# VectorE makes ten low parts of weight tiles around four norms, three output stages use 256-column triples, and two latent statistics share one PSUM bank

## The chip, the cores and the metric

The kernel runs on one core of one Trainium2 chip. The metric is device time in microseconds, from several runs of the whole program; the profile is one further execution, recorded by the hardware profiler.

## The reference

Two transformer blocks over one sequence of 256 tokens with 1024 channels, all in 32-bit floating point. What matters here:

```python
def rms_norm(x, g, eps=1e-6):
    y = x * rsqrt(mean(x * x, axis=-1) + eps)
    return y * g

# first_block, for l in 0, 1 (l = 0: convolution and memory attention, l = 1: NSA and memory attention)
x = x + mix @ w_out[l]
x = x + square(relu(rms_norm(x, norm_mlp_g[l]) @ w_mlp_in[l])) @ w_mlp_out[l]     # 1024 -> 4096 -> 1024
# at l = 1, from x: kv = rms_norm(x, kv_norm_g) @ w_kv, and h = rms_norm(x, norm_mix_g[1])

# second_block
proj = rms_norm_2(x, g_pre_mix) @ w_in
sb_q, sb_k, sb_v, q_lat, kv_lat, k_rope = split(proj)           # q_lat: 256 channels, kv_lat: 128
o_sb = stick_breaking_attention(sb_q, sb_k, sb_v)
q = rms_norm_2(q_lat, g_q_lat) @ w_q_up
kv = rms_norm_2(kv_lat, g_kv_lat) @ w_kv_up
# MLA attention, output projection, a convolved GELU MLP, and a gated embedding follow
```

## The kernel before

**Layout.** Channels lie on partitions, tokens along the free dimension: x is 8 tiles of 128 channels by 256 tokens. A weight matrix is read in blocks of 1 MB into a ring of four (SyncE's queue); a block holds two weight tiles, each of which gives 128 output channels from up to 8 k-steps. WEIGHT_TILES numbers them through the kernel; they are 280.

**Exact products from parts.** Each fp32 operand is split into a high part, rounded to fp32r, and a low part, the rest. ScalarE makes a weight tile's high part (`split_high`, L618); the low part is a subtraction of 128x1024 elements (`split_low`, L626) on VectorE or GpSimd, as LOW_ENGINE, made by `low_part_engines`, says. Four slots (SPLIT) of parts are in flight: the parts of tile w + 4 are made once TensorE is through with tile w; `pump(stage, t)` stands in the queues of ScalarE and VectorE for that. GpSimd makes its own with `low_parts` in the order of the tiles.

**Two forms of a k-step on TensorE.** `linear` issues a triple of 256-column matmuls: high x high, high x low, low x high (`product`). `linear_halves` issues two: the high weights against both parts of the activation side by side (512 columns), and the low weights against the high part (256 columns); the output then stands in two halves of the bank that have to be added (`half_products`).

**Banks.** Six PSUM banks are used in turn, in the order of `psum_tiles()`: tile n takes bank n mod 6 once tile n - 6 has been emptied. All matmuls are recorded at L758 (`mm`), transposes at L928.

**The four norms.** Behind out0, mlp_out0, out1 and mlp_out1 an RMS norm of x follows (mlp0, mix1, mlp1, smix), whose factor is put in behind the next product. `residual` on VectorE goes through the 8 output tiles:

```python
                for t in range(KD):
                    add_output(stage, first + t)
                    if t >= 1:
                        low_of_x(t - 1, hi, lo, gname, name)
                        fold(name, t - 1)
                        pump(stage, first + t - 1)
                low_of_x(KD - 1, hi, lo, gname, name)
                fold(name, KD - 1)
                pump(stage, first + KD - 1)
```

add_output adds the two halves to x's tile; ScalarE (`squares_of_x`) then makes the tile's high part and its square and runs its own pump; low_of_x makes the low part, for which the next stage's first tile waits k-step by k-step (`linear(..., arriving)`); fold sums the squares. Between chunks the MLP's back products (mlp_out tiles 0 to 23) use add_output as well. After two tiles of the next stage TensorE sums the squares into the statistic, ScalarE takes the root, VectorE the reciprocal, TensorE broadcasts it.

**The latent stage.** Behind the stick sums (`stick_sums`) TensorE makes s_lat 0 (the kv latent), the statistic of the q latent, s_lat 1 (the rotary key), the statistic of the kv latent, the first token half of s_val 0, and both broadcasts, then a swap of the rotary key, the second token half, and the query heads. ScalarE has the logs of four heads (a table load for Ln), pumps and squares, then two roots (another table load); VectorE has `stick_keeps`, the scaled latents and two reciprocals (`invert`). The query heads wait until VectorE has read the q latent's broadcast.

Of the kernel before, what the change touches and what calls it, by code (L numbers as in the profile page):

```python
# [218 lines left out]
def psum_tiles():  # L219
# [110 lines left out]
        linear("s_in", 1, t)  # L330
    linear("sb.Z", 1, 7)
    linear("sb.C", 4)
    linear("s_lat", 1)
    linear("qlat.stat", 1)
    linear("s_lat", 1, 1)
    linear("kvlat.stat", 1)
    linear("qlat.bc", 1)
    linear("kvlat.bc", 1)
    linear("krope.swap", 1)
# [69 lines left out]


GATE_SUMMED = 14
ON_GPSIMD = (("ple_gate", 2), ("ple_gate", 3))


def low_part_engines():

    out = []
    for w, (_, _, (stage, t)) in enumerate(WEIGHT_TILES):
        beside_conv = w >= SPLIT and (stage in ("a_in", "mem_kv0", "mem_kv1") or (stage == "out0" and t < 2))
        beside_sticks = w % 2 == 1 and (stage in ("s_lat", "s_val") or (stage == "s_in" and t >= SPLIT))  # L420
        out.append("gpsimd" if beside_conv or beside_sticks or (w >= SPLIT and w % 4 == 1 and stage not in ("b_in", "up") and (stage, t) != ("out0", 3)
                                                             and (stage, t) != ("ple_gate", 1))
                   or (stage, t) in ON_GPSIMD else "vector")
    return out

# [11 lines left out]
def build(nc, x_in, mem_in, p_in, pos_in, consts_in, weights_in, out):  # L437
    ctx = ExitStack()
    with ctx:
# [304 lines left out]
        def _(pe):  # L744
# [390 lines left out]
            def mlp(name, into, back, signal, sizes, per, act):  # L1135
                for n in range(len(sizes) + 1):
                    if n == 0 and per == 2:
                        dst = take(f"{name}.stat", 0)
                        for k in range(KD):
                            arriving_squares(name, dst, k)  # L1140
                        full_bcast(name)
                        linear(into, 0, sizes[0] * per, act, f"{name}.act")
                    elif n == 0:
                        linear_halves(into, 0, 2, act, f"{name}.act")
                        folded_stat(name)
                        linear_halves(into, 2, 1, act)
                        full_bcast(name)
                        linear_halves(into, 3, sizes[0] * per - 3, act)
                    elif n < len(sizes) and per == 1:
                        linear_halves(into, KD * n * per, sizes[n] * per, act)  # L1150
                    elif n < len(sizes):
                        linear(into, KD * n * per, sizes[n] * per, act)
                    if n >= 1:

                        pe.wait_ge(sem(signal), KD * (n - 1) + sizes[n - 1])
                        linear_halves(back, KD * (n - 1), KD, hidden_parts[:, :, (n - 1) % 2, :, :])

            def block_ready(name, r=0):
                b = BLOCK_AT[name, r, 0]
# [212 lines left out]
                    wait_out_emptied(pe, ("nsa", tt, g))  # L1372
            for tt in range(TT):
                wait_out_emptied(pe, ("mem1", "mem", tt, 0))
            linear_halves("out1", 0, KD, act_parts)
            mlp_block(1)


# [63 lines left out]
            pe.wait_ge(sem("sb.below"), 1)  # L1442
            for h in range(4):
                stick_sums(h)
            linear("s_lat", 0, 1, projected)
            full_stat("qlat", 2, signal=1)
            linear("s_lat", 1, 1, projected)
            full_stat("kvlat", 1, src=sq[:, 2:3, :], signal=1)
            linear_tokens("s_val", 0, 2, projected, (0,))
            full_bcast("qlat")  # L1450
            full_bcast("kvlat")
# [108 lines left out]
        def _(act):  # L1560
# [437 lines left out]
            for t in range(2):  # L1998
                wait_emptied(act, "s_in", 8 + t)
            do(flat(sq[:, 0:2, :]), flat(lat[:, 0:2, :]), ACT.Square).then_inc(sem("qlat.squares"), 1)  # L2000
            stick_logs(range(4, 8))
            pump("s_lat", 0)
            wait_emptied(act, "s_lat", 0)
            do(sq[:, 2, :], lat[:, 2, :], ACT.Square).then_inc(sem("kvlat.squares"), 1)
            pump("s_lat", 1)
            root("qlat", 2, 256)
            root("kvlat", 2, 128)
            token_pair("s_val", 0, sbv[:, :, 0:256], "smix")
            keep_queries(range(4))
            stick_weights(range(4, 8))  # L2010
# [207 lines left out]
        def _(dve):  # L2218
# [48 lines left out]
                stt(lo[:, t, :], x[:, t, :], const(gname, t, 1), hi[:, t, :].bitcast(F32), ALU.mult, ALU.subtract)\  # L2267
                    .then_inc(sem(f"{name}.act"), 1)

            def add_output(stage, t):  # L2270
                wait_tile(dve, stage, t)
                settle(tt_(x[:, t % KD, :], x[:, t % KD, :], bank(stage, t)[:, 0:SEQ], ALU.add))
                tt_(x[:, t % KD, :], x[:, t % KD, :], bank(stage, t)[:, SEQ:2 * SEQ], ALU.add).then_inc(emptied(stage, t), 1)

# [20 lines left out]
            def residual(stage, first, hi, lo, gname, name):  # L2295

                for t in range(KD):
                    add_output(stage, first + t)
                    if t >= 1:
                        low_of_x(t - 1, hi, lo, gname, name)  # L2300
                        fold(name, t - 1)
# [4 lines that stand above are left out]
# [631 lines left out]
            pump("s_lat", 0)  # L2937
            stick_keeps((4, 5))
            scaled(("s_lat", 1), krope[64:96, :], bank("s_lat", 1)[64:96, 0:SEQ], rb[64:96, :])
            pump("s_lat", 1)  # L2940
            invert("qlat", 2)
            invert("kvlat", 2)
            stick_keeps((6, 7))
            wait_tile(dve, "qlat.bc", 0)
            for t in range(2):
# [370 lines left out]
```

## Time and profile before

| | |
|---|---|
| runs, median | 1050.36 us |
| runs, lowest and highest of 3 | 1049.38, 1052.92 us |
| profiled execution | 1048.86 us, of which span 1047.0 us |
| TensorE matmul busy | 989.5 us (95%) |
| VectorE busy | 783.5 us (75%) |
| ScalarE busy | 610.1 us (58%) |
| GpSimd busy | 205.7 us (20%) |
| mean granted clock of TensorE | 0.982 |
| low parts (L626) | 206 on VectorE, 74 on GpSimd |

Shares are of the span. A matmul row's duration reaches over the start of the next one, because matmuls are pipelined: the distance from start to start is the pace, and the duration is longer. The same holds, less, for VectorE and ScalarE. In a timeline an idle time in brackets is that of the engine before the row, with what ended it. The granted clock is 1.00 at 2.4 GHz and 0.50 at 1.2 GHz.

### The profile page before, as it was taken

To read this page: it belongs to the slowest core of one execution; us is meant where nothing else is said; L and a number is where in the kernel's file an instruction comes from. 1 tells how busy PE (TensorE), PEld (TensorE's weight loads), DVE (VectorE), ACT (ScalarE), POOL (GpSimd) and SP (SyncE) were. 2 spreads that over 40 slices of the span, in tenths; PEclk is the share of its full clock that TensorE was granted. 3 is DMA by queue.
4 is the path that set the end of the run, shared out by engine and by line. 5 is a ranking of instruction groups with operands and counts; after the bars stand their busy time and mean duration, and the time that the engine had idled before them with its cause. 6 is when DMAs were issued, how large, how long until landed. Compare 5 with 4: busy or idle time off the path is not lost.

```text
span 1047.0 us, 17720 instructions
## 1 busy us (share of the span) xinstructions
PE 989.5 (95%) x6807; PEld 885.7 (85%) x6807; DVE 783.5 (75%) x1446; ACT 610.1 (58%) x1143; POOL 205.7 (20%) x109
## 2 busy tenths in 40 slices
PE   4999999999999996899999999999999999999986
PEld 4978888888889885788878888897798999999875
DVE  4888789876868768877987677666576788768775
ACT  5634557564645867645547455574565665545555
POOL 2953112122111001001212211222000000202151
PEclk9999999999999999999999999998998999999998
DMA  9481154555544440034455454521405354554601
GB/s 379 168 239 57 66 201 162 203 200 176 190 176 183 167 161 1 1 142 167 175 201 201 166 202 162 197 85 46 161 6 197 122 190 176 203 187 154 219 1 41
DMA packets 24995, 160.49 MB, mean 153 GB/s; under 512 B 2768, under 2 KB 5072, under 8 KB 6608
## 3 DMA queue, kind: packets, MB, share of 16 engines
q1 hardware_dynamic: 24048, 155.69, 41.1%
q10 hardware_dynamic: 864, 3.66, 0.9%
q8 instruction: 55, 0.90, 0.4%
q14 instruction: 28, 0.23, 0.1%
HBM read 157.86 MB, written 1.49 MB: 152 GB/s over the span
## 4 chain that ended last, share of the span: by engine, by line
PE 77%; DVE 14%; ACT 4%; issue 4%; DMA 1%; DVEq 0%; ACTq 0%
PE bank L758 73%; DVE split_lo L626 2%; PE obank L758 2%; PE bank L928 1%; ACT split_hi L618 1%; DVE tmp L2240 1%; DVE mlp_parts L2240 1%; DMA consts<-in_consts 1%; DVE x L2232 1%; DVE rowmax L2790 1%; ACT L1570 1%; DVE hidden_parts L2232 1%; DVE tmp L2232 1%; DVE act_parts L2232 1%; DVE probs L2236 0%
## 5 line engine op out<-in xcount | busy, mean ns | idle before, releaser
L618 ACT ACTIVATE split_hi<-ring 128x1024 fp32r<-128x1024 f32 (+1 forms) x280 | 290.0, 1049 | 117.4 <-PE bank L758 116.9
L758 PE MATMUL bank<-act_parts,split_hi 128*128 128x256 f32 (+1 forms) x1632 | 317.8, 293 | 23.0 <-DVE split_lo L626 13.4
L626 POOL TENSOR_TENSOR split_lo<-ring,split_hi 128x1024 fp32r<-128x1024 f32 (+1 forms) x74 | 180.6, 2450 | 704.0 <-ACT split_hi L618 703.9
L758 PEld LDWEIGHTS bank<-act_parts,split_hi 128*128 128x128 f32 x1632 | 256.4, 191 | 33.1 <-issue 24.2
L626 DVE TENSOR_TENSOR split_lo<-ring,split_hi 128x1024 fp32r<-128x1024 f32 (+1 forms) x206 | 250.7, 1227 | 41.0 <-ACT split_hi L618 40.3
L758 PE MATMUL bank<-hidden_parts,split_hi 128*128 128x512 f32 (+1 forms) x816 | 267.1, 379 | 5.5 <-DVE split_lo L626 2.5
L758 PE MATMUL bank<-act_parts,split_lo 128*128 128x256 f32 x880 | 247.8, 282 | 0.0
L758 PE MATMUL bank<-hidden_parts,split_lo 128*128 128x256 f32 x752 | 210.8, 280 | 0.0
L758 PEld LDWEIGHTS bank<-hidden_parts,split_hi 128*128 128x128 f32 x816 | 149.8, 189 | 37.5 <-DVE split_lo L626 3.1
L758 PE MATMUL bank<-mlp_parts,split_hi 128*128 128x512 f32 x512 | 178.8, 392 | 2.1 <-DVE mlp_parts L2240 2.1
L758 PEld LDWEIGHTS bank<-act_parts,split_lo 128*128 128x128 f32 x880 | 167.4, 190 | 0.0
L758 PE MATMUL bank<-mlp_parts,split_lo 128*128 128x256 f32 x512 | 144.3, 282 | 0.0
L758 PEld LDWEIGHTS bank<-hidden_parts,split_lo 128*128 128x128 f32 x752 | 141.8, 189 | 0.0
L758 PEld LDWEIGHTS bank<-mlp_parts,split_hi 128*128 128x128 f32 x512 | 96.1, 188 | 23.0 <-DVE mlp_parts L2240 2.9
L758 PEld LDWEIGHTS bank<-mlp_parts,split_lo 128*128 128x128 f32 x512 | 96.8, 189 | 0.0
L2232 DVE TENSOR_TENSOR x<-x,bank 128x256 f32<-128x256 f32 x160 | 67.0, 419 | 37.7 <-PE bank L758 34.4
L2240 DVE SCALAR_TENSOR_TENSOR tmp<-bank,consts,tmp 128x255 f32<-128x255 f32 (+1 forms) x88 | 39.7, 476 | 29.3 <-ACT tmp L1570 29.2
L2232 DVE TENSOR_TENSOR tmp<-bank,tmp 128x256 f32<-128x256 f32 x64 | 27.0, 422 | 37.9 <-ACT tmp L1573 35.4
L1570 ACT ACTIVATE tmp<-bank,consts 128x256 f32<-128x256 f32 x45 | 25.3, 563 | 47.2 <-PE bank L758 47.1
L1570 ACT ACTIVATE tmp<-tmp 128x256 f32<-128x256 f32 x64 | 26.8, 418 | 28.5 <-DVE tmp L2240 26.2
L2232 DVE TENSOR_TENSOR hidden_parts<-tmp,hidden_parts 128x256 fp32r<-128x256 f32 x64 | 41.3, 660 | 0.0
L1570 ACT ACT_TABLE_LOAD x29 | 37.2, 1283 | 4.3 <-issue 3.8
(285 smaller groups left out, 1245.5 us busy)
## 6 DMA issues: line engine op xcount, KB each, us to landing
ring<-in_weights SPq DMA_DIRECT2D x141, 1024.0 KB, 4.8
ring<-in_weights SPq DMA_DIRECT2D x5, 768.0 KB, 4.3
shifted<-conv_rows SPq DMA_DIRECT2D x9, 142.0 KB, 4.4
x<-in_x ACTq DMA_DIRECT2D x1, 1024.0 KB, 7.8
y<-in_mem ACTq DMA_DIRECT2D x1, 1024.0 KB, 9.8
out<-x SPq DMA_DIRECT2D x4, 256.0 KB, 2.6
consts<-in_consts ACTq DMA_DIRECT2D x1, 933.0 KB, 13.1
ring<-in_weights SPq DMA_DIRECT2D x1, 512.0 KB, 3.5
```

Of the source, the lines that this page charges most:

```text
L618: nc.scalar.activation(split_hi[:, w % SPLIT, 0:n], src, ACT.Copy).then_inc(sem("high_parts"), 1)
L626: (nc.vector if engine == "vector" else nc.gpsimd).tensor_tensor(split_lo[:, w % SPLIT, 0:n], src, split_hi[:, w % SPLIT, 0:n].bitcast(F32 ...
L758: return nc.tensor.matmul(dst, lhsT, rhs, start=start, stop=stop)
L928: return nc.tensor.transpose(dst, src, const("ident")[0:k, 0:k])
L1570: return nc.scalar.activation(dst, src, func, bias=bias, scale=scale, **more)
L2232: return nc.vector.tensor_tensor(dst, a, b, op)
L2240: return nc.vector.scalar_tensor_tensor(out=dst, in0=a, scalar=s, in1=b, op0=op0, op1=op1)
L2790: settle(nc.vector.reduce_max(rowmax[:, c:c + m], bank("nsa", "S", n)[:, :].rearrange("p (s k) -> p s k", k=u.keys), X_AXIS, negate=True))
```

## The change

Three edits. (1) Ten weight tiles near the four norms get their low part from VectorE instead of GpSimd. (2) out1 and the last eight tiles of mlp_out0 and mlp_out1 are made as 256-column triples (`linear`), and the add on VectorE is a single one there; out0 and the other tiles of mlp_out keep the halves. (3) Both latent statistics are written to one bank behind s_lat 1, as four columns; ScalarE squares the kv latent before the logs; both roots follow one wait, and both reciprocals stand before pump("s_lat", 1). psum_tiles() has one tile fewer, so that the banks of all later tiles shift by one.

```diff
-    linear("s_lat", 1)
-    linear("qlat.stat", 1)
-    linear("s_lat", 1, 1)
-    linear("kvlat.stat", 1)
+    linear("s_lat", 2)
+    linear("lat.stat", 1)
...
+LAST_BACK = KD * (len(MLP_CHUNKS) - 1)
+BESIDE_NORMS = {(stage, t) for l in range(2) for stage, first, n in ((f"out{l}", 4, 4), (f"mlp_in{l}", 0, 4), (f"mlp_out{l}", LAST_BACK, 8))
+                for t in range(first, first + n)} | {(stage, t) for stage in ("kv", "s_in") for t in range(4)}
...
+        beside_norms = (stage, t) in BESIDE_NORMS
...
-                                                             and (stage, t) != ("ple_gate", 1))
+                                                             and (stage, t) != ("ple_gate", 1) and not beside_norms)
...
-                        linear_halves(back, KD * (n - 1), KD, hidden_parts[:, :, (n - 1) % 2, :, :])
+                        if per == 1 and n == len(sizes):
+                            linear(back, KD * (n - 1), KD, chunk_of((n - 1) % 2))
+                        else:
+                            linear_halves(back, KD * (n - 1), KD, hidden_parts[:, :, (n - 1) % 2, :, :])
...
-            linear_halves("out1", 0, KD, act_parts)
+            linear("out1", 0, KD, projected)
...
-            linear("s_lat", 0, 1, projected)
-            full_stat("qlat", 2, signal=1)
-            linear("s_lat", 1, 1, projected)
-            full_stat("kvlat", 1, src=sq[:, 2:3, :], signal=1)
+            linear("s_lat", 0, 2, projected)
+            pe.wait_ge(sem("qlat.squares"), 1)
+            pe.wait_ge(sem("kvlat.squares"), 1)
+            dst = take("lat.stat", 0)
+            for tt in range(TT):
+                for k in range(3):
+                    c = 2 * (k // 2) + tt
+                    last = mm(dst[:, c:c + 1], sq[:, k, 128 * tt:128 * tt + 128], const("ones", 0, 1), k != 1, k >= 1)
+            ready(last)
...
             do(flat(sq[:, 0:2, :]), flat(lat[:, 0:2, :]), ACT.Square).then_inc(sem("qlat.squares"), 1)
+            wait_emptied(act, "s_lat", 0)
+            do(sq[:, 2, :], lat[:, 2, :], ACT.Square).then_inc(sem("kvlat.squares"), 1)
             stick_logs(range(4, 8))
             pump("s_lat", 0)
-            wait_emptied(act, "s_lat", 0)
-            do(sq[:, 2, :], lat[:, 2, :], ACT.Square).then_inc(sem("kvlat.squares"), 1)
             pump("s_lat", 1)
-            root("qlat", 2, 256)
-            root("kvlat", 2, 128)
+            wait_tile(act, "lat.stat", 0)
+            for n, (name, dim) in enumerate((("qlat", 256), ("kvlat", 128))):
+                c = RC[name]
+                ins = do(smalls[:, c:c + 2], bank("lat.stat", 0)[:, 2 * n:2 * n + 2], ACT.Sqrt, const("eps6"), 1.0 / dim)
+                if n:
+                    ins.then_inc(emptied("lat.stat", 0), 1)
...
-            def add_output(stage, t):
+            def add_output(stage, t, whole=False):
                 wait_tile(dve, stage, t)
+                if whole:
+                    tt_(x[:, t % KD, :], x[:, t % KD, :], bank(stage, t)[:, 0:SEQ], ALU.add).then_inc(emptied(stage, t), 1)
+                    return
                 settle(tt_(x[:, t % KD, :], x[:, t % KD, :], bank(stage, t)[:, 0:SEQ], ALU.add))
                 tt_(x[:, t % KD, :], x[:, t % KD, :], bank(stage, t)[:, SEQ:2 * SEQ], ALU.add).then_inc(emptied(stage, t), 1)
...
-                    add_output(stage, first + t)
+                    add_output(stage, first + t, stage != "out0")
...
             scaled(("s_lat", 1), krope[64:96, :], bank("s_lat", 1)[64:96, 0:SEQ], rb[64:96, :])
+            wait_emptied(dve, "lat.stat", 0)
+            for name in ("qlat", "kvlat"):
+                assert inverted[inversions[0]] == name
+                inversions[0] += 1
+                nc.vector.reciprocal(rc[:, RC[name]:RC[name] + 2], smalls[:, RC[name]:RC[name] + 2]).then_inc(sem("inverted"), 1)
             pump("s_lat", 1)
-            invert("qlat", 2)
-            invert("kvlat", 2)
             stick_keeps((6, 7))
```

## Rows read from the trace of the kernel before

**Rows 1.** The page's part 4, shares of the chain by engine.
```profile
PE 77%; DVE 14%; ACT 4%; issue 4%; DMA 1%; DVEq 0%; ACTq 0%
```

**Rows 2.** TensorE's timeline, the first matmul after each norm's wait: start, duration.
```profile
145.37 0.50 PE L758 MATMUL bank<-mlp_parts,split_hi 128*128 128x512 f32 x1 [0.83 <-DVE mlp_parts L2240]
...
325.82 0.39 PE L758 MATMUL bank<-hidden_parts,split_hi 128*128 128x256 f32 x1 [0.72 <-DVE hidden_parts L2240]
...
477.58 0.50 PE L758 MATMUL bank<-mlp_parts,split_hi 128*128 128x512 f32 x1 [1.25 <-DVE mlp_parts L2240]
...
661.88 0.51 PE L758 MATMUL bank<-act_parts,split_hi 128*128 128x256 f32 x2 [1.24 <-DVE act_parts L2240]
```

**Rows 3.** The latent stage: timelines of TensorE, ScalarE, VectorE, and a window (the clock is PEclk).
```profile
710.42 0.55 PE L758 MATMUL bank<-split_hi,act_parts 128*128 128x256 f32 x1 [2.00 <-ACT smalls L1570]
...
715.68 1.33 PE L758 MATMUL bank<-consts,rc 128*128 128x128 f32 x8
...
720.48 3.62 PE L758 MATMUL bank<-temps,ring 128*96 128x256 f32 x16
...
703.44 1.28 ACT L1570 ACT_TABLE_LOAD   x1
...
707.36 0.40 ACT L1570 ACTIVATE sq<-temps 128x256 f32<-128x256 f32 x1
...
710.02 0.41 ACT L1570 ACTIVATE smalls<-bank,consts 128x2 f32<-128x2 f32 x2
...
703.48 0.42 DVE L2232 TENSOR_TENSOR temps<-bank,rb 128x256 f32<-128x256 f32 x1 [1.13 <-PE bank L758]
...
709.10 2.71 DVE L2240 SCALAR_TENSOR_TENSOR decays<-sq,decays 128x384 f32<-128x384 f32 x1
...
714.01 0.23 DVE L2249 RECIPROCAL rc<-smalls 128x2 f32<-128x2 f32 x2
...
709.43:716.26 6.83, 5.84 (x27) 5.87 (x28) 6.63 (x13) 0.99 (x3) 1.96 (x1) 0.50 0.42 154
```

**Rows 4.** VectorE's timeline, last tile of mlp_out0.
```profile
322.63 0.88 DVE L2232 TENSOR_TENSOR x<-x,bank 128x256 f32<-128x256 f32 x2
323.42 0.48 DVE L2240 SCALAR_TENSOR_TENSOR hidden_parts<-x,consts,hidden_parts 128x256 fp32r<-128x256 f32 x1
323.82 0.42 DVE L2232 TENSOR_TENSOR square_sum<-square_sum,sq 128x256 f32<-128x256 f32 x1
324.15 1.22 DVE L626 TENSOR_TENSOR split_lo<-ring,split_hi 128x1024 fp32r<-128x1024 f32 x1
325.29 0.48 DVE L2240 SCALAR_TENSOR_TENSOR hidden_parts<-x,consts,hidden_parts 128x256 fp32r<-128x256 f32 x1
```

**Rows 5.** TensorE's timeline, last matmul of a k-step: first and last of 65, 51 and 47 steps.
```profile
452.33 0.28 PE L758 MATMUL bank<-act_parts,split_lo 128*128 128x256 f32 x1
...
474.86 0.28 PE L758 MATMUL bank<-mlp_parts,split_lo 128*128 128x256 f32 x1
...
304.11 0.28 PE L758 MATMUL bank<-hidden_parts,split_lo 128*128 128x256 f32 x1
...
321.96 0.28 PE L758 MATMUL bank<-hidden_parts,split_lo 128*128 128x256 f32 x1
...
776.12 0.28 PE L758 MATMUL bank<-act_parts,split_lo 128*128 128x256 f32 x1
...
792.73 0.28 PE L758 MATMUL bank<-act_parts,split_lo 128*128 128x256 f32 x1
```

**Rows 6.** VectorE's and GpSimd's timelines, tile 6 of the last mlp_out1 chunk.
```profile
656.21 2.22 DVE L2240 SCALAR_TENSOR_TENSOR act_parts<-x,consts,act_parts 128x256 fp32r<-128x256 f32 x1
...
655.75 2.40 POOL L626 TENSOR_TENSOR split_lo<-ring,split_hi 128x1024 fp32r<-128x1024 f32 x1 [9.18 <-ACT split_hi L618]
```

**Rows 7.** TensorE's wait behind the feed-forward norm, and the window behind it.
```profile
1006.92 0.77 PE L758 MATMUL bank<-act_parts,split_hi 128*128 128x256 f32 x2 [4.51 <-DVE act_parts L2240]
...
1006.40:1009.80 3.40, 2.88 (x13) 2.91 (x14) 3.40 (x7) 2.56 (x9) 2.59 (x4) 0.50 0.00 0
```

## The prediction

> **What bounds the kernel.** I read first the chain that ended last, by engine: TensorE holds 77% of it and VectorE 14% [rows 1]. So work moved between VectorE and GpSimd counts only where TensorE waits for it, and I looked next at TensorE's timeline at the five places that the diff touches. Around each of the four norms TensorE stops once, at the same place: the last of the eight k-steps of the first tile behind the norm waits for the low part of x's tile 7. The waits are 0.83, 0.72, 1.25 and 1.24 us [rows 2], 4.04 us together: more than that the norms cannot give, 0.4% of the kernel. In the latent stage it waits once for 2.00 us, for the square root of the first statistic [rows 3].
>
> **Why the norms' waits have two sizes.** VectorE's timeline at the end of the first block's MLP is the undisturbed case [rows 4]. The two halves of x += output start at 322.63, low_of_x(6) at 323.42, the fold of squares at 323.82, the low part of a weight tile (pump) at 324.15, low_of_x(7) at 325.29, and TensorE goes on at 325.82. The adds thus take 0.79 us of VectorE's queue, a low_of_x 0.40, a fold 0.33, a weight tile's low part 1.14: 2.66 us a tile. TensorE, without a wait, would have gone on 0.72 earlier, at 325.10. A tile of TensorE is 8 steps of 0.347 us in out1 [rows 5], 2.77 us, so VectorE has only 0.11 us a tile with which to catch up. At the end of the second MLP it is disturbed [rows 6]: GpSimd's low part starts at 655.75, the low_of_x issued at 656.21 lasts 2.22 us instead of 0.48 and ends with it. Both of its tensor operands lie in SBUF, as do GpSimd's. That iteration has no pump, so the net loss is 1.74 - 1.14 = 0.60 us, two tiles before the end, and 0.11 a tile cannot repay it. Thus 1.24 instead of 0.72.
>
> **Low parts moved to VectorE.** By the rule in low_part_engines ten tiles change sides: out0 7, mlp_in0 3, mlp_out0 27 and 31, kv 3, out1 5, mlp_in1 1, mlp_out1 25 and 29, s_in 1. Each costs VectorE 1.14 us [rows 4], 11.4 us in all, and takes a GpSimd piece of 2.4 us away [rows 6]. Hardly any of it is on the path alone: mlp_out0 27 and mlp_out1 25 fall into an iteration in which VectorE has time to spare, mlp_in0 3, kv 3 fall behind low_of_x(7), where the next thing that TensorE wants from VectorE is two tiles away; the rest each replace a stall, 1.74 us in the one shown, by 1.14.
>
> **One add instead of two.** With triples the product is whole in columns 0 to 255 and add_output is one operation: 0.33 us of the queue, as the fold shows [rows 4], instead of 0.79, so 0.46 saved on the last tile of three stages, and the iteration falls to 2.20 us against TensorE's 2.77: VectorE then meets every tile as it ends, and nothing that happened earlier is left at the end. For the three triple stages the wait is then 0.72 - 0.46 = 0.26 us. What remains is the pump of tile 6, which stands in VectorE's queue ahead of low_of_x(7); the triples don't move it. Savings: 0.46 at mlp_out0, 0.99 at out1, 0.98 at mlp_out1. out0 keeps its halves, and only loses its stall: 0.83 to 0.72, 0.11. Together 2.54 us. If VectorE does not catch up in any of them, the stages save only the 0.46 each, 1.4 us; the other bound is the whole 4.04.
>
> **Triples on TensorE.** Both forms stream 768 columns a step, but three matmuls and three weight loads instead of two of each. 24 tiles of 8 steps are 192 steps. Halves in out1: 452.33 to 474.86 for 65 steps, 0.3467 us; halves in mlp_out0: 304.11 to 321.96 for 51, 0.3500; triples in o: 776.12 to 792.73 for 47, 0.3533 [rows 5]. Low bound: nothing, since the columns are the same. High bound, all at o's pace: 64 x 0.0066 + 128 x 0.0033 = 0.85 us. I take 0.5, about the middle, since the halves' own pace varies between stages by as much as the difference.
> The Trainium skill ("TensorE: Matmul & The Clock Gate", section "Wait — 56ns, not 53.3ns?") speaks against this edit: each matmul costs about 2.5 ns beyond its columns. By that, as an estimate, 192 more matmuls would cost 0.48 us. The difference of 3.3 to 6.6 ns a step between the rows is of that order.
>
> **The latents.** Before [rows 3]: s_lat 0, its statistic, s_lat 1, its statistic, and then s_val waits for a bank that the root of qlat.stat empties at 710.02, behind a table load. With the new numbering s_val 0 takes the bank of s_lat 0, which VectorE empties at once. So TensorE runs on: s_lat 1 from 703.3, where s_lat 0 ends (VectorE picks it up at 703.48), with no statistic in front, until 706.1; six one-column products for some 0.8 us (eight broadcast products take 1.33), s_val's first half of 2.85 us (24 matmuls at 0.118 us, a third of o's step [rows 5]) to about 709.8. Then it needs the reciprocals. ScalarE now squares the kv latent before the logs, and for that waits until VectorE has scaled s_lat 0 (703.48 + 0.42 = 703.90): with the square's 0.40 the logs' table load starts at 704.3, 0.85 us later than 703.44; the square taken out behind them gives about 0.3 back. All that follows on ScalarE is 0.55 us later: the high part that frees GpSimd's s_val 3, and the roots. On VectorE the stall behind that GpSimd piece (2.71 us at 709.10) ends 0.55 later too, and the reciprocals move from 714.01 to about 714.56. Behind the waiting reciprocals only stick_keeps((6, 7)) is queued, which is wanted after 720. The broadcast starts at 714.66 instead of 715.68, and to the query heads it is as before 4.80 us (715.68 to 720.48), less 0.29 for the half clock that ended in it: 719.2, a gain of 1.3 us.
> But TensorE is then idle for 4.9 us, and comes back cold. In the stage before the clock was granted at 0.50 from 709.43 to 716.26, behind a pause of 2 us [rows 3]; behind a later wait of 4.51 us until 1006.92, it was 0.50 (1.2 GHz) until 1009.8, 2.88 us busy [rows 7]. Half of 2.88, 1.44 us, is what that stretch costs; where it starts earlier, about 1 us. I take 1.3: gain and loss cancel, latents 0. Bounds: -1.3 with the clock full, +1.0 if two stretches follow (4.6 us of work at half).
>
> **Sum.** Against the profiled execution, 1048.86 us (span 1047.0): -2.54 + 0.5 + 0.0 = -2.0, so 1046.8. It ran 1.5 us below the median of the runs shown, 1050.36; against that, 1048.3 us.
>
> **Rivals.** 1. *The moved wait costs more than the removed one.* TensorE's one pause of 4.9 us brings two slow stretches; latents +1.0, total -1.0: 1049.3. For it: one pause of 2 us already had a slow stretch twice as long as the one at 1006.4. Against it: the longer pause there had only one. The same page of the Trainium skill, section "Why this matters for your kernels", warns of long pauses between bursts of matmuls, because the clock falls; by it the removal of a 2 us wait is not worth a pause of 4.9. The trace agrees that it falls.
> 2. *The clock stays up*, or the slow stretch falls into the pause. Latents -1.3, total -3.3: 1047.0. Against it: both pauses shown, of 2.00 and of 4.51 us, have a slow stretch behind them.
> 3. *Slower than before.* The slow stretch starts just as TensorE comes back and is as long as before, 6.83 us, all of it over dense products: it costs 3.4 instead of 1.3, latents +2.1; with the triples at their high bound (+0.85) the total is -2.54 + 0.85 + 2.1 = +0.4: 1050.8. It decides from a slow stretch of about 6 us of work on; two unlucky ones also elsewhere would be needed to pass +0.3%.
> 4. *VectorE is not what holds the norms.* If low_of_x(7) waits for ScalarE's high part, or the waits come back in the next tile, the four give only the triples' cost: total +0.5: 1050.9. Against it: all four waits are ended by VectorE's low_of_x [rows 2], which follows on its pump without a gap [rows 4].
>
> **How the numbers follow.** Forecast 0.45, rival 1 0.2, rival 2 0.15, rival 3 0.08, rival 4 0.12. 0.3% is 3.15 us, about what a measurement of this kernel tells from no change; the three runs before spread over 3.5 us. Faster by more means below 1047.2: rival 2 mostly, and the lower end of the forecast (norms at their 4.04 bound), 0.25. Slower by more, above 1053.5, needs rival 3 or 4 and an execution with more slow stretches: 0.1. The same: 0.65. The range goes from the forecast with 4.04 for the norms and -1.0 for the latents (1050.36 - 4.5 = 1045.8) to rivals 3 and 4, 1051.0. The forecast's own range is 1047.0 to 1049.6.
>
> **What would show it.** Right: the norms' waits in TensorE's timeline at 0.2 to 0.4 us in three, 0.7 in the first; no VectorE operation of over 1.3 us in the four stages but the low parts; GpSimd with 64 instead of 74 low parts; the step of the triples at 0.350 to 0.354; in the latent stage no wait between the statistic and s_val, one wait of 4 to 5.5 us before the broadcast, and a slow clock behind it. Wrong: if the wait behind out1 stays above 1 us (then VectorE doesn't catch up), if the steps exceed 0.357 (then the third weight load is not hidden), or if the reciprocals come after 716.

## The result, and the profile after

| | before | after |
|---|---|---|
| median of 12 runs each | 1050.36 us | 1054.47 us |
| lowest and highest | 1048.20, 1052.92 | 1052.36, 1056.58 |
| ratio, 95% interval | | 1.0043 [1.0034, 1.0052] |
| profiled execution (span) | 1048.86 (1047.0) | 1054.04 (1052.2) |
| mean granted clock of TensorE | 0.982 | 0.978 |
| low parts on VectorE, on GpSimd | 206, 74 | 216, 64 |

The changed kernel is slower by 4.1 us, and lies outside the predicted range. The profiled executions differ by 5.2 us.

First the part of the page that the prediction began with, the shares of the chain, after (TensorE had 77% in [rows 1]):

```profile
PE 81%; DVE 11%; ACT 3%; issue 3%; DMA 1%; DVEq 0%; ACTq 0%
```

TensorE's share of the chain has risen by 4 points, and by the two pages its matmuls are busy for 996.8 us where they were for 989.5. It is idle for 2 us less and still takes longer: the time is lost while TensorE works.

**The norms.** TensorE's timeline, the first matmul after each norm's wait, after:

```profile
146.22 0.50 PE L760 MATMUL bank<-mlp_parts,split_hi 128*128 128x512 f32 x1 [0.81 <-DVE mlp_parts L2254]
...
326.85 0.50 PE L760 MATMUL bank<-hidden_parts,split_hi 128*128 128x256 f32 x2 [0.26 <-DVE hidden_parts L2254]
...
478.06 0.50 PE L760 MATMUL bank<-mlp_parts,split_hi 128*128 128x512 f32 x1 [0.34 <-DVE mlp_parts L2254]
...
662.02 0.50 PE L760 MATMUL bank<-act_parts,split_hi 128*128 128x256 f32 x2 [0.32 <-DVE act_parts L2254]
```

They were 0.83, 0.72, 1.25 and 1.24 [rows 2], 4.04 us; now 1.73. The waits give back 2.31 us. VectorE's timeline at the end of the second MLP shows why, against [rows 4, 6]:

```profile
659.28 0.42 DVE L2246 TENSOR_TENSOR x<-x,bank 128x256 f32<-128x256 f32 x1 [0.59 <-PE bank L760]
659.62 0.48 DVE L2254 SCALAR_TENSOR_TENSOR act_parts<-x,consts,act_parts 128x256 fp32r<-128x256 f32 x1
660.02 0.42 DVE L2246 TENSOR_TENSOR square_sum<-square_sum,sq 128x256 f32<-128x256 f32 x1
660.35 1.22 DVE L628 TENSOR_TENSOR split_lo<-ring,split_hi 128x1024 fp32r<-128x1024 f32 x1
661.49 0.48 DVE L2254 SCALAR_TENSOR_TENSOR act_parts<-x,consts,act_parts 128x256 fp32r<-128x256 f32 x1
```

The single add starts 0.59 us after VectorE ran dry: it waits for the tile to end. There is one add where two stood, and the low part of a weight tile (660.35, the pump of tile 6) is what is left ahead of low_of_x(7).

**The triples' steps.** TensorE's timeline, last matmul of a k-step, after: first and last of 55 steps in mlp_out0, 65 in out1 and 49 in mlp_out1.

```profile
303.99 0.28 PE L760 MATMUL bank<-hidden_parts,split_lo 128*128 128x256 f32 x1
...
323.80 0.28 PE L760 MATMUL bank<-hidden_parts,split_lo 128*128 128x256 f32 x1
...
452.95 0.28 PE L760 MATMUL bank<-act_parts,split_lo 128*128 128x256 f32 x1
...
475.70 0.28 PE L760 MATMUL bank<-mlp_parts,split_lo 128*128 128x256 f32 x1
...
641.33 0.28 PE L760 MATMUL bank<-hidden_parts,split_lo 128*128 128x256 f32 x1
...
658.97 0.28 PE L760 MATMUL bank<-hidden_parts,split_lo 128*128 128x256 f32 x1
```

The steps are 0.3602, 0.3500 and 0.3600 us; as halves they were 0.3500 in mlp_out0 and 0.3467 in out1 [rows 5], and 0.3500 in mlp_out1 too (before, 640 to 657 us). That is 128 x 0.010 + 64 x 0.0033 = 1.5 us, where the prediction had 0.5 and a high bound of 0.85. Waits and steps together: a gain of 0.8 us.

**The latents.** TensorE's, ScalarE's and VectorE's timelines after, and windows over two stretches at the lower clock (busy time of the engines, then the granted clock, DMA share and GB/s):

```profile
715.37 2.05 PE L760 MATMUL bank<-consts,rc 128*128 128x128 f32 x8 [4.84 <-DVE rc L2961]
...
722.76 2.54 PE L760 MATMUL bank<-temps,ring 128*96 128x256 f32 x11
...
704.06 0.42 ACT L1580 ACTIVATE sq<-temps 128x256 f32<-128x256 f32 x1 [0.53 <-DVE temps L2246]
704.49 1.28 ACT L1580 ACT_TABLE_LOAD   x1
...
710.76 0.41 ACT L1580 ACTIVATE smalls<-bank,consts 128x2 f32<-128x2 f32 x2
...
703.60 0.42 DVE L2246 TENSOR_TENSOR temps<-bank,rb 128x256 f32<-128x256 f32 x1 [1.15 <-PE bank L760]
...
708.53 1.23 DVE L628 TENSOR_TENSOR split_lo<-ring,split_hi 128x1024 fp32r<-128x1024 f32 x1 [4.51 <-ACT split_hi L620]
709.67 2.71 DVE L2254 SCALAR_TENSOR_TENSOR decays<-y,decays 128x384 f32<-128x384 f32 x1
...
715.06 0.23 DVE L2961 RECIPROCAL rc<-smalls 128x2 f32<-128x2 f32 x2
...
714.70:721.50 6.80, 6.13 (x24) 5.23 (x25) 5.65 (x15) 0.00 (x0) 0.78 (x1) 0.50 0.21 88
...
769.40:776.20 6.80, 6.80 (x35) 6.80 (x34) 3.38 (x11) 2.60 (x6) 0.00 (x0) 0.50 0.01 2
```

The pause before the broadcast is there, 4.84 us, as worked out. But the broadcast starts at 715.37, not 714.66, and the query heads at 722.76, not 719.2; before they started at 720.48 [rows 3]. From the broadcast to the heads it takes 7.39 us, where it took 4.80. The slow stretch begins as the pause ends (714.70) and TensorE is busy for 6.13 of its 6.80 us; in [rows 3] it began at 709.43. A second one of 6.80 us lies in the output projection, all of it dense products. No window at half clock lay there in the profiled execution of before.

Laid matmul by matmul against the profiled execution of before, TensorE is late by

| at (us, before) | 100 | 690 | 730 | 760 | 830 | 1002 |
|---|---|---|---|---|---|---|
| late by (us) | 0.9 | 0.1 | 2.3 | 2.3 | 4.4 | 5.1 |

The 0.9 us stand there before the first tile that the diff touches, and the profiled executions of the other kernels below lie between -0.5 and +0.9 us there, so they are not the change's. From 100 to 690 the norms and steps give the 0.8 us back that their rows give. The latent stage loses 2.2 us and the output projection 2.1, and 0.7 come in the feed-forward block, whose code is unchanged but for the numbers of the banks. Its steps are 0.3533 us in a part of it where they were 0.3500, as they are in the profiled execution of e9 below too, which has before's banks.

### The profile page after: what moved, and what is told of

Same layout as the page of the kernel before. It is cut to its first block, busy times and chain, and to the rows that moved or that the text cites. A ratio compares the mean times of both kernels' runs of the same rounds, so it can differ in the third digit from the quotient of the medians.

```text
span 1052.2 us, 18079 instructions
## 1 busy us (share of the span) xinstructions
PE 996.8 (95%) x6999; PEld 901.5 (86%) x6999; DVE 770.6 (73%) x1432; ACT 610.3 (58%) x1143; POOL 181.4 (17%) x99
## 4 chain that ended last, share of the span: by engine, by line
PE 81%; DVE 11%; ACT 3%; issue 3%; DMA 1%; DVEq 0%; ACTq 0%
PE bank L760 78%; PE obank L760 3%; DVE split_lo L628 2%; PE bank L930 1%; DVE tmp L2254 1%; DMA consts<-in_consts 1%; DVE rowmax L2807 1%; DVE hidden_parts L2246 1%; DVE tmp L2246 1%; ACT split_hi L620 1%; DVE probs L2250 0%; DVE pt_lo L2246 0%; ACT L1580 0%; DVE y L2246 0%; ACT probs L1580 0%
## 5 line engine op out<-in xcount | busy, mean ns | idle before, releaser
L760 PE MATMUL bank<-act_parts,split_hi 128*128 128x256 f32 (+1 forms) x1696 | 321.3, 290 | 21.9 <-DVE split_lo L628 13.3
L628 DVE TENSOR_TENSOR split_lo<-ring,split_hi 128x1024 fp32r<-128x1024 f32 (+1 forms) x216 | 262.7, 1225 | 44.5 <-ACT split_hi L620 43.9
L760 PEld LDWEIGHTS bank<-act_parts,split_hi 128*128 128x128 f32 x1696 | 266.2, 192 | 29.1 <-issue 24.1
L628 POOL TENSOR_TENSOR split_lo<-ring,split_hi 128x1024 fp32r<-128x1024 f32 (+1 forms) x64 | 155.8, 2445 | 697.1 <-ACT split_hi L620 696.9
L760 PEld LDWEIGHTS bank<-hidden_parts,split_hi 128*128 128x128 f32 x944 | 165.1, 189 | 31.4 <-DVE split_lo L628 3.1
L2246 DVE TENSOR_TENSOR x<-x,bank 128x256 f32<-128x256 f32 x136 | 57.0, 419 | 45.5 <-PE bank L760 43.2
```

The lines of the kernel that those rows point to most:

```text
L628: (nc.vector if engine == "vector" else nc.gpsimd).tensor_tensor(split_lo[:, w % SPLIT, 0:n], src, split_hi[:, w % SPLIT, 0:n].bitcast(F32 ...
L760: return nc.tensor.matmul(dst, lhsT, rhs, start=start, stop=stop)
L2246: return nc.vector.tensor_tensor(dst, a, b, op)
```

## The experiments

In each, "mean" is the mean time of the runs compared; before, in the same batches, had medians of 1050.16, 1050.04 and 1050.81 us and means of 1050.23, 1050.22 and 1050.78 us (29 to 35 runs each). Each of the three batches is compared with its own, and the change with the 12 runs of before beside it (mean 1050.30); the differences below are of means. Such a difference is uncertain by about 1 us either way, e1's by 2.

**One part at a time: e1 (edit 3), e2 (edits 1 and 2), e3 (edit 1), e9 (edit 2).** The edits are hunks of the diff above, put on the kernel before. e9, as it differs from the kernel before (the hunk of mlp_out and the body of add_output are as above):

```diff
...
-            linear_halves("out1", 0, KD, act_parts)
+            linear("out1", 0, KD, projected)
...
-                    add_output(stage, first + t)
+                    add_output(stage, first + t, stage != "out0")
```

> The kernel before with the third edit alone (both latent statistics in one bank). Theory A: the latent edit is where the time went. TensorE's pause of 5 us before the broadcast brings a slow stretch of 6.8 us over dense products, and a further slow stretch follows in the output projection (from 769 us in the changed kernel); together 2.1 + 2.3 us and a little more behind it: 4 to 5.5 us over before, ratio 1.004 to 1.005. Rival B: the further slow stretch is chance of one execution or comes of the norm edits; then only the 2.1 us of the latent stage, ratio about 1.002. Rival C: the latents cost nothing and the norm edits are to blame: 1.000.

> The kernel before with the first two edits alone (low parts on VectorE, triples), old latent stage. Theory A: the waits shrink from 4.04 to about 1.7 us and the triples give 1.5 us back (0.360 instead of 0.350 us a step in both mlp_out stages, 0.350 instead of 0.347 in out1), so 0.6 to 0.9 us under before, ratio 0.999 to 1.000. Rival C: the norm edits are to blame, ratio above 1.002.

> The kernel before with the first edit alone: ten low parts on VectorE, halves everywhere. The waits behind out1 and mlp_out1 fall from 1.25 to about 0.72 us, since no GpSimd piece stalls VectorE there, and no triple costs anything: 1.1 us under before, ratio 0.999, and at least as good as with the triples. If VectorE does not catch up with two adds a tile, the waits stay near 1.2 and the ratio at 1.000.

> Edit 2 alone (triples in out1 and the last eight tiles of both mlp_outs; the ten low parts stay on GpSimd, the latent stage is the old one). Theory (the stalls behind GpSimd's pieces and the two half adds were separate costs that add up; the triples' steps cost 1.3 us at 0.360 and 0.2 us at 0.350): the norms' waits 0.83, 0.26, about 0.3 to 0.8 and 0.8, since with 0.57 us to spare a tile VectorE catches up one stall of 1.7 us only in three tiles; total -1.9 + 1.5 = -0.4 us, 1049.8. Rival (triples are the whole gain of the two edits, low parts give nothing): same waits as with both edits, 0.83, 0.26, 0.34, 0.32, total -0.8 or better, since the ten low parts don't cost VectorE anything: 1049.3. Second rival (the triples' slower steps eat more than the waits give): above 1050.5.

| | median us | ratio [95%] | mean, less before's |
|---|---|---|---|
| e1, latents | 1055.53 | 1.0042 [1.0025, 1.0059] | +4.3 |
| e2, low parts and triples | 1048.98 | 0.9993 [0.9984, 1.0002] | -0.8 |
| e3, low parts | 1051.11 | 1.0005 [0.9996, 1.0015] | +0.5 |
| e9, triples | 1050.67 | 1.0001 [0.9988, 1.0014] | 0.0 |
| the change (its own 12 runs of before) | 1054.47 | 1.0043 [1.0034, 1.0052] | +4.2 |

The latent edit alone makes the kernel as slow as the whole change does. Edits 1 and 2 come out as the 0.8 us that the profile's rows give, though the interval still holds 1, so that they gain anything isn't shown. e1's figures rest on six runs, and its profiled one is the fastest of them (1051.39, clock 0.981); its slowest took 1056.84 at 0.976. The clocks differ by 0.005. As the clock has two levels, 1.00 and 0.50, that is 10.5 us more of the 1050 at half clock; half of it, 5.25, is nearly the 5.45 us between the two. TensorE's wait and a window in e1's trace:

```profile
715.17 2.05 PE L756 MATMUL bank<-consts,rc 128*128 128x128 f32 x8 [4.84 <-DVE rc L2951]
```

```profile
713.50:723.70 10.20, 8.53 (x36) 7.58 (x37) 6.62 (x17) 0.11 (x1) 1.88 (x1) 0.52 0.22 93
```

The same pause, and a slow stretch of 10.2 us. It begins at 713.0, half a microsecond ahead of the window shown, so TensorE is busy for some 8 us of it. e1's trace, laid against before's, loses 2.9 us in the latent stage and nothing more up to 805, with the banks numbered as in the change: that shift costs nothing there.

TensorE's norm waits in e3:

```profile
145.95 0.51 PE L762 MATMUL bank<-mlp_parts,split_hi 128*128 128x512 f32 x1 [0.81 <-DVE mlp_parts L2244]
...
326.41 0.50 PE L762 MATMUL bank<-hidden_parts,split_hi 128*128 128x256 f32 x2 [0.72 <-DVE hidden_parts L2244]
...
477.84 0.50 PE L762 MATMUL bank<-mlp_parts,split_hi 128*128 128x512 f32 x1 [0.81 <-DVE mlp_parts L2244]
...
661.63 0.51 PE L762 MATMUL bank<-act_parts,split_hi 128*128 128x256 f32 x2 [0.78 <-DVE act_parts L2244]
```

and in e9, with VectorE's and GpSimd's operations at tile 6 of the last mlp_out1 chunk:

```profile
145.82 0.50 PE L758 MATMUL bank<-mlp_parts,split_hi 128*128 128x512 f32 x1 [0.83 <-DVE mlp_parts L2243]
...
326.45 0.50 PE L758 MATMUL bank<-hidden_parts,split_hi 128*128 128x256 f32 x2 [0.26 <-DVE hidden_parts L2243]
...
477.14 0.50 PE L758 MATMUL bank<-mlp_parts,split_hi 128*128 128x512 f32 x1 [0.36 <-DVE mlp_parts L2243]
...
661.45 0.50 PE L758 MATMUL bank<-act_parts,split_hi 128*128 128x256 f32 x2 [0.32 <-DVE act_parts L2243]
...
656.17 2.07 DVE L2243 SCALAR_TENSOR_TENSOR act_parts<-x,consts,act_parts 128x256 fp32r<-128x256 f32 x1
...
655.55 2.40 POOL L626 TENSOR_TENSOR split_lo<-ring,split_hi 128x1024 fp32r<-128x1024 f32 x1 [9.42 <-ACT split_hi L618]
```

Either edit removes what the stalls left: the low parts alone take the waits to 0.72 to 0.81, the triples alone to 0.26 to 0.36, with the stall of 2.07 us still there. With the single add VectorE has time to repay it before the last tile. Beside the triples the ten low parts give 0.04 us of waits (1.77 against 1.73). The low parts for themselves save 4.04 - 3.12 = 0.92 us of waits, but the runs of e3 don't show it: +0.5, and its interval, down to 0.9996, excludes a gain of 0.92 us. What took it back is open. e9's waits and steps give 0.8 us by the rows, and its runs 0.0, which is within their uncertainty.

**e8: the triples in out1 only,** with edit 1 (mlp_out keeps its halves: the step of 0.360 and its 1.3 us go). As it differs from e2:

```diff
-                        if per == 1 and n == len(sizes):
-                            linear(back, KD * (n - 1), KD, chunk_of((n - 1) % 2))
-                        else:
-                            linear_halves(back, KD * (n - 1), KD, hidden_parts[:, :, (n - 1) % 2, :, :])
+                        linear_halves(back, KD * (n - 1), KD, hidden_parts[:, :, (n - 1) % 2, :, :])
...
-                    add_output(stage, first + t, stage != "out0")
+                    add_output(stage, first + t, stage == "out1")
```

> The kernel before with the first edit and triples in out1 alone; mlp_out keeps its halves. If the dear step (0.360 instead of 0.350 us) belongs to the triples of mlp_out, the two last mlp_out chunks give 1.3 us back and cost 0.46 us each in longer waits: 0.3 to 0.4 us under the two norm edits together (0.9993), ratio 0.998 to 1.000. If the step stays at 0.360 there, it has another cause.

1050.39 us, 1.0004 [0.9992, 1.0016], mean +0.2. The halves of mlp_out are back at 0.350 us a step, but the waits behind them at 0.72 and 0.78. What the step costs and what the wait gives (1.3 us against 0.92) lie too close for the runs to tell them apart: e8 was expected below e2 and isn't, and it settles nothing more.

**e4: the pause filled with the kernel's own work.** On the changed kernel, both token halves of s_val 0 stand ahead of the broadcasts.

```diff
+    linear("s_val", 1)
...
-    linear("s_val", 1)
...
-            linear_tokens("s_val", 0, 2, projected, (0,))
+            linear_tokens("s_val", 0, 2, projected)
...
-            linear_tokens("s_val", 0, 2, projected, (1,))
```

> The changed kernel with the second token half of s_val 0 moved ahead of the broadcasts (and its bank taken there), so that 2.9 us of products stand in TensorE's pause of 5 us. Theory A: the pause falls to about 2 us, another of 1.5 to 2 us stands before the query heads, which start 2 us earlier than in the kernel before, and the long slow stretch shrinks or goes: 3 to 6 us under the changed kernel, ratio 0.997 to 1.000. Rival B (the stretch in the output projection is not tied to the pause): 2 to 3 us under it, ratio 1.001 to 1.002. Rival C: no change from the changed kernel, 1.004.

1050.64 us, 1.0004 [0.9996, 1.0013]; mean +0.1, so 4.1 us less than the change. TensorE's timeline and a window of e4:

```profile
713.46 1.13 PE L760 MATMUL bank<-consts,rc 128*128 128x128 f32 x8 [2.04 <-DVE rc L2960]
716.98 5.05 PE L760 MATMUL bank<-temps,ring 128*96 128x256 f32 x16 [1.79 <-DVE temps L2253]
```

```profile
716.40:719.80 3.40, 2.82 (x7) 1.96 (x8) 3.20 (x7) 0.38 (x1) 0.99 (x1) 0.51 0.00 0
```

TensorE does the same work and still stands for 3.83 us, instead of 4.84, but in two pieces of 2, and the lower clock lasts 3.40 us instead of 6.80. One microsecond less of waiting comes with 4 us less of time; the rest is put down to the clock, for which the means over all runs below speak too.

**e5 and e6: the pause filled with work that nobody needs.** 20 products of 512 columns (bf16, constant operands) go into the bank of the broadcast before it is made; e5 has edit 3 alone, e6 is the whole change. The work of the kernel is unchanged.

```diff
-                if name in ("ffn", "postffn", "postple"):
-                    keep_busy(dst, {"postple": 3 * (1 - again)}.get(name, 4))
+                if name in ("ffn", "postffn", "postple", "qlat"):
+                    keep_busy(dst, {"postple": 3 * (1 - again), "qlat": 20}.get(name, 4))
```

> The kernel before with the latent edit alone, and 20 needless 512-column products of constants in TensorE's pause before the q broadcast (about 4.4 us at full clock; they write the bank that the broadcast then overwrites). Theory A: the pause is what lowers the clock, and the slow stretches behind it, not the pause, are what the edit costs. With TensorE occupied the clock stays at 1.00 from 707 to 720, the query heads start 1 to 1.5 us earlier than before, and the runs come to 0 to 2 us under before, 4 to 6 us under the latent edit alone (1.0042): ratio 0.998 to 1.000. Rival D: the latent edit costs time by its later chain (reciprocals and what waits for them): the ratio stays at 1.003 to 1.004 although the clock is full.

> The changed kernel with the same 20 needless products in the pause. Theory A: the norm edits' gain (0.8 us in the mean) comes on top: 1 to 2.5 us under before, ratio 0.9975 to 0.999. Rival D: 1.003 to 1.004, as the changed kernel.

| | median us | ratio [95%] | mean, less before's | the same without the fill |
|---|---|---|---|---|
| e5 | 1052.51 | 1.0021 [1.0007, 1.0035] | +1.9 | +4.3 (e1) |
| e6 | 1050.32 | 0.9999 [0.9988, 1.0010] | -0.1 | +4.2 (the change) |

TensorE's timeline in e5, and windows of e6:

```profile
711.36 4.49 PE L756 MATMUL bank<-cbias_b,ident_b 128*128 128x512 bf16 x20
716.27 1.16 PE L756 MATMUL bank<-consts,rc 128*128 128x128 f32 x8 [0.42 <-DVE rc L2951]
```

```profile
710.30:715.20 4.90, 4.58 (x23) 1.92 (x21) 4.77 (x9) 0.88 (x3) 1.69 (x1) 1.00 0.39 139
715.20:722.00 6.80, 6.70 (x44) 5.75 (x45) 5.26 (x15) 1.87 (x4) 1.26 (x1) 1.00 0.13 55
765.50:772.30 6.80, 6.80 (x34) 6.80 (x34) 3.36 (x11) 2.59 (x5) 0.00 (x0) 0.50 0.00 0
```

Twenty products that serve nothing take 4.3 us off the whole change, clearly, and 2.4 off the latent edit, only just beyond the runs' uncertainty. Both kernels were expected below before's time, and neither is. The products end no wait earlier: the broadcast of e6 starts at 715.30, 0.07 from where it did without them. Only the clock differs, 1.00 where it was 0.50, and from the broadcast to the query heads e6 takes 4.63 us and e5 4.62, where the change took 7.39:

```profile
719.93 3.62 PE L760 MATMUL bank<-temps,ring 128*96 128x256 f32 x16
```

The last window shows what the fill doesn't reach, the slow stretch in the output projection.

**What the new order is worth at full clock.** Against the profiled execution of before, TensorE passes the latent stage (690 to 730) 0.7 us sooner in e6 and in e5. But that execution is the odd one. In those of e2, e3, e8, e9 and e10, whose latent stage is the same as before's, the slow stretch behind the same pause lasted 3.40 us instead of 6.83, and the stage passed 1.1 us sooner than in before's. e2's, as an example:

```profile
709.35 0.43 PE L762 MATMUL bank<-split_hi,act_parts 128*128 128x256 f32 x1 [2.01 <-ACT smalls L1577]
...
709.50:712.90 3.40, 3.40 (x17) 3.40 (x18) 3.30 (x6) 0.00 (x0) 0.82 (x1) 0.50 0.36 104
```

Against these five the new order gains nothing by 730 even with its pause filled, and unfilled it loses 3.3 us in the profile of the change and 4.1 in e1's, not 2.2 and 2.9.

**e7: the stall beside GpSimd's s_val 3 taken away.** On the changed kernel VectorE makes the low part of s_val 3, behind the reciprocals.

```diff
-        beside_sticks = w % 2 == 1 and (stage in ("s_lat", "s_val") or (stage == "s_in" and t >= SPLIT))
+        beside_sticks = w % 2 == 1 and (stage, t) != ("s_val", 3) and (stage in ("s_lat", "s_val") or (stage == "s_in" and t >= SPLIT))
...
-                                                             and (stage, t) != ("ple_gate", 1) and not beside_norms)
+                                                             and (stage, t) not in (("ple_gate", 1), ("s_val", 3)) and not beside_norms)
```

> The changed kernel with the low part of s_val 3 made by VectorE (behind the reciprocals) instead of GpSimd, so that no GpSimd piece holds up stick_keeps((4, 5)) in front of the reciprocals. The reciprocals come 2 us earlier and TensorE's pause falls from 5.0 to about 3 us. Theory A: both the chain and the cold clock get shorter, 2 to 4 us under the changed kernel, ratio 1.000 to 1.002. If the clock falls for a pause of 3 us as for one of 5, only 1 to 2 us: 1.002 to 1.003.

1050.96 us, 1.0013 [1.0000, 1.0026]; mean +1.3, so 2.9 us less than the change. TensorE's timeline and a window:

```profile
714.84 1.13 PE L760 MATMUL bank<-consts,rc 128*128 128x128 f32 x8 [2.68 <-DVE rc L2961]
```

```profile
716.40:719.80 3.40, 3.40 (x16) 3.05 (x16) 3.30 (x8) 0.00 (x0) 0.00 (x0) 0.53 0.77 277
```

Without the stall of 2.71 us the pause shrinks by 2.16 us, and 3.40 us at the lower clock follow in place of 6.80. The time falls by 2.9 us, which is the pause's 2.16 within the runs' uncertainty.

**The clock over all runs.** Each run has a mean granted clock, and with levels of 1.00 and 0.50 it gives the time at the lower one. As an estimate, that time costs half of itself at most, where all of it falls on dense products. The runs compared here are of different batches in part.

| | mean clock | us at the lower clock |
|---|---|---|
| before, in the three batches | 0.9796, 0.9801, 0.9792 | 42.7, 41.8, 43.6 |
| the change; e1; e7 | 0.9769; 0.9775; 0.9768 | 48.6; 47.4; 48.6 |
| e4; e5; e6 | 0.9800; 0.9805; 0.9815 | 41.9; 41.1; 38.7 |

e6 has 9.9 us less of it than the change, at most 5.0 us of time (measured 4.3); e5 6.3 less than e1, at most 3.1 (2.4); e4 6.7 less than the change, 3.4 and the wait's 1.0 together 4.4 (4.1). e7 has no less than the change: over all its runs only the shorter pause is seen. e1 has 4.7 us more than before, at most 2.4 of its 4.3 us; the rest fits a slow stretch that fell partly into the pause before and falls on dense products now. e5 has no more than before, so its +1.9 us are not explained by longer slow stretches.

**e10 and e11: a second fill.** 28 dummy products instead of 10 ahead of the gate (ple_gate, the first product behind the feed-forward norm), where TensorE stood for 4.51 us [rows 7]; e10 on e2, e11 on e6.

```diff
-            keep_busy(take("ple_gate", 0), 10)
+            keep_busy(take("ple_gate", 0), 28)
```

> Edits 1 and 2 with the old latent stage, and 28 instead of 10 dummy products of 512 columns (0.22 us each) ahead of the first gate product, where TensorE otherwise stands for about 4.5 us at about 1002. They are the candidate for the fastest version. Theory (what a pause costs is the slow clock over the dense work behind it): the slow stretch at about 1003 to 1007 goes, half of 2.9 us of busy time at half clock is saved, -1.4 us against the 1048.98 of the two edits alone: 1047.6 by the median. Rival (the clock falls for another reason, or the fill ends later than VectorE's low part and delays the product): no change or up to +0.5, 1049 to 1049.5.

> The changed kernel with both fills: 20 dummy products in the latent stage's pause of 5 us and 28 instead of 10 ahead of the gate. Theory: 1050.3 of the changed kernel with the first fill alone, less 1.4 us for the clock behind the second: 1048.9; it stays 0.5 to 1.5 us above the version with the old latent stage and the same second fill. Rival (the latents' new order is worth what was hoped once no clock is lost): at or below that version.

| | median us | ratio [95%] | mean, less before's |
|---|---|---|---|
| e10 | 1049.99 | 0.9991 [0.9979, 1.0002] | -0.9 |
| e11 | 1048.52 | 0.9985 [0.9973, 0.9998] | -1.9 |

TensorE's timeline in e11, and windows:

```profile
999.42 6.21 PE L760 MATMUL bank<-cbias_b,ident_b 128*128 128x512 bf16 x28
1006.27 0.47 PE L760 MATMUL bank<-act_parts,split_hi 128*128 128x256 f32 x2 [0.64 <-DVE act_parts L2254]
```

```profile
714.20:722.00 7.80, 7.77 (x49) 6.55 (x50) 6.26 (x14) 2.94 (x6) 1.95 (x2) 1.00 0.12 51
1006.27:1013.07 6.80, 6.71 (x53) 6.30 (x54) 6.80 (x10) 3.70 (x10) 5.55 (x6) 1.00 0.00 0
```

Behind both former pauses the clock is full, where [rows 7] show 0.50. e11 is the one version whose interval lies wholly below before's time, by 0.15%. The two give the second fill a different worth: e10 is at e2's difference (-0.9 against -0.8), where 1.4 less were expected, e11 1.8 us below e6's; but that is within the uncertainty of four means. e11's place against e10 (1.0 us lower) is within what these runs leave uncertain.

## Why the prediction was wrong

**The norms' waits: right in the trace.** Predicted 0.72 and three of 0.26, measured 0.81, 0.26, 0.34 and 0.32: 2.31 us instead of 2.54. The reason for the single add was right too (VectorE meets every tile as it ends). That a stall makes the difference between 0.7 and 1.25 was right as well: e3, without stalls but with two adds, waits 0.81 and 0.78 there. What the sum gave to the low parts on top of the single add was not theirs: e9 has nearly the same waits without them.

**The triples' steps: mis-sized.** 0.5 was taken and 0.85 was the high bound, from the step of o. Measured is 1.5 us, nearly all of it at 0.360 us a step in mlp_out, above the mark of 0.357 at which the prediction called itself wrong. That mark stood for a third weight load that isn't hidden; whether that is the cause wasn't tested, and the same form runs at 0.350 in out1. The Trainium skill's 2.5 ns for each matmul ("TensorE: Matmul & The Clock Gate", section "Wait — 56ns, not 53.3ns?"), weighed in the prediction, would have been too little as well: a step of one more matmul is 10 ns longer in mlp_out and 3.3 in out1.

**The latents: the step that failed.** "I take 1.3: gain and loss cancel, latents 0." The wait of 4.9 us was right (4.84). The start of the reciprocals was 0.5 late (715.06, not 714.56): the 0.3 us that taking out the later square gives back never reaches VectorE, whose unbroken chain from the low part at 708.53 to the reciprocals (6.53 us, before 6.52) starts behind the weight tile ahead of that square. The broadcast follows them by 0.31 us, not 0.10. Then the size of the slow stretch, which is the greater part. The prediction took its cost, 1.3, from the 2.88 us of busy time behind the later pause [rows 7], though the row for this very stage had a stretch of 6.83 [rows 3]. Measured are stretches of 6.80 and 10.20 us over dense products. From the broadcast to the heads the change takes 7.39 us and e6, at full clock, 4.63, so the clock costs 2.8, and the stage stands 2.2 us behind where it stood before, beyond the upper bound of 1.0. That is rival 3's mechanism, and its figure for this stage (+2.1). It had a chance of 0.08, because it was tied to the triples' high bound and to a stretch longer than the one of [rows 7]; yet the triples passed that bound, and the length stood in [rows 3]. The Trainium skill's warning of long pauses between bursts of matmuls (same page, section "Why this matters for your kernels"), named there beside rival 1, agrees with what the runs show here: 4.3 us between the pause and the same pause filled.

**The sum.** With what was measured it is -2.3 + 1.5 + 2.2 = +1.4, not -2.0: that alone would have made the kernel slower, but only by about a quarter of what the profiles differ by (5.2). The rest of that, 0.9 at the start, 2.1 in the output projection and 0.7 in the feed-forward block, stands where the diff changes nothing, or nothing but the numbers of the banks, and no term had it. The sum also leaned on one execution of before whose latent stage was 1.1 us slower than in the five other profiles with the same stage.

**Shown and not shown.** Shown: the latent edit is the loss (e1 against e2), and the slow clock behind the pause is most of it (e6: idle time replaced by dummy products, the wait's end unmoved, -4.3 us; e5 and e4 support it, e7 doesn't bear on the clock). That e1's 4.3 us are the latent stage's alone fits its profile, 4.1 us against the five others, but with one profile of it that is argued. Not shown: what the slow stretch in the output projection has to do with the edit. Stretches of 6.8 us that begin between 764.3 and 769.4 are in the profiled executions of the change, e5, e6 and e7, but also of e3, e8, e9 and e10, which have the old latent stage; they are not in those of e1, e4, e2 and before, and e11 has one earlier, at 751.2. So they depend on the execution, and whether the latent edit makes them more frequent is open. Open is also why e5, at full clock and 0.7 us ahead in its stage, is still 1.9 us slower than before; its profiled execution has that stretch and one of 10.2 us at 806.7, but over all runs it is no longer at the lower clock than before is. e6 lies 0.8 us above e2 too. With its pause filled the latent edit still seems to cost something, and what, apart from the 0.4 us by which its stage passes later than in the five other profiles, wasn't found.

## What to carry to other kernels

Before a wait is moved, add up what TensorE will do at half clock behind it, and take the length of the slow stretch from the rows of that very stage, not from the kindest one, and from more than one execution; one pause of 5 us ahead of dense products cost more than the 2 us wait that it replaced. Where such a pause can't be shortened, filling it with real products (e4) or with dummy ones (e6) gave 4 us back. And where two edits attack one wait, run each alone: here one of them did all of the waits' work.

## What the hardware did that was not expected

Behind a pause of 2.00 us the lower clock lasted 6.83 us in the profiled execution of before [rows 3] and 3.40 us in the five others with that stage and that pause (2.01 us). Behind one of 4.84 us it lasted 6.80 us in the change and 10.20 in e1, and behind the pauses of e4 (2.04 and 1.79 us) and e7 (2.68) 3.40: the pause's length alone doesn't give it. The same triple of 256-column products took 0.359 to 0.360 us in mlp_out0 and mlp_out1 in the profiled executions of the change, e2, e4, e6, e7 and e9 to e11, and in out1 0.350 in those of the change, e2, e4 and e9 to e11, but 0.353 in those of e6 to e8.
